# A two-block transformer step on one core: attention products turned round into two column groups, a reciprocal spread by a matmul, x read in four transfers, the constants waited for later

## The reference, cut to what matters

```
    def one_block(qblk):
        s = jnp.concatenate([jnp.einsum('bgrqd,bgkd->bgrqk', qblk, k),
                             jnp.einsum('bgrqd,bgcd->bgrqc', qblk, kc)], axis=-1)
        p = jax.nn.softmax(s.astype(jnp.float32) * scale, axis=-1).astype(v.dtype)
        return (jnp.einsum('bgrqk,bgkd->bgrqd', p[..., :length], v)
                + jnp.einsum('bgrqc,bgcd->bgrqd', p[..., length:], vc))
    ...
    y = _merge_heads(_dense_attention(q[:, :, None], k, v, kc, vc, MLA_SCALE)[:, :, 0]) @ w_out
```

## Time and profile before

| | us |
|---|---|
| median of 3 runs | 1869.68 (1869.36 to 1870.29) |
| the profiled execution | 1873.88 |
| its span between first and last instruction | 1872.0 |
| PE busy | 1694.2 (91%) |
| DVE busy | 951.4 (51%) |
| ACT busy | 743.0 (40%) |
| POOL busy | 101.9 (5%) |

### The profile page before, as it was taken

One profiled execution on the slowest core, in us unless ns is written; L12 is line 12 of the kernel. 1 busy time (PEld: TensorE's weight loads), 2 busy tenths in 40 slices (PEclk: granted clock), 3 DMA queues, 4 the chain that ended last, 5 costly groups with the idle time before them and its releaser, 6 DMA issues.

```text
span 1872.0 us, 36381 instructions
## 1 busy us (share of the span) xinstructions
PE 1694.2 (91%) x14713; PEld 1372.9 (73%) x14713; DVE 951.4 (51%) x1734; ACT 743.0 (40%) x1398; POOL 101.9 (5%) x158
## 2 busy tenths in 40 slices
PE   6888899897798887999998999999998799989997
PEld 6776578686566665877775887888786657779997
DVE  4743563476623224274555655245535555468584
ACT  5332434454111124224654433333326325565454
POOL 0020000004000001000002100000011000010000
PEclk9989899998899999999998999999998899989999
DMA  6597676668599997221002222323222310235552
GB/s 231 181 225 278 225 250 236 228 227 254 228 388 408 407 369 257 79 79 46 1 26 77 78 97 89 98 91 98 83 97 68 101 51 1 91 124 183 182 188 68
DMA packets 84799, 303.57 MB, mean 162 GB/s; under 512 B 10080, under 2 KB 12128, under 8 KB 84512
## 3 DMA queue, kind: packets, MB, share of 16 engines
q1 hardware_dynamic: 80576, 290.49, 44.3%
q0 software_dynamic: 2736, 7.35, 1.7%
q10 hardware_dynamic: 1328, 3.47, 0.5%
HBM read 347.14 MB, written 3.15 MB: 187 GB/s over the span
## 4 chain that ended last, share of the span: by engine, by line
PE 79%; DVE 9%; ACT 4%; DMA 4%; issue 4%; SPq 0%; ACTq 0%; DVEq 0%
PE bank L926 50%; PE bank L871 15%; PE bank L1403 4%; DMA ring<-wall 3%; PE bank L1438 3%; PE bank L1423 3%; PE bank L950 3%; DVE w_lo L2099 1%; ACT w_hi L1629 1%; DVE BIG L2722 1%; DMA con<-consts 1%; PE bank L1415 1%; PE bank L1459 1%; ACT BIG L1692 0%; DVE BIG L2395 0%
## 5 line engine op out<-in xcount | busy, mean ns | idle before, releaser
L926 PE MATMUL bank<-BIG_f32r,w_hi 128*128 128x256 f32 (+1 forms) x2208 | 550.7, 339 | 23.9 <-DVE BIG_f32r L2114 15.8
L2099 DVE TENSOR_TENSOR w_lo<-ring,w_hi 128x1024 fp32r<-128x1024 f32 x260 | 322.7, 1250 | 331.1 <-ACT w_hi L1629 329.7
L926 PEld LDWEIGHTS bank<-BIG_f32r,w_hi 128*128 128x128 f32 x2208 | 381.5, 192 | 73.6 <-issue 25.6
L926 PE MATMUL bank<-BIG_f32r,w_lo 128*128 128x256 f32 (+1 forms) x1136 | 385.9, 340 | 0.0
L1629 ACT ACTIVATE w_hi<-ring 128x1024 fp32r<-128x1024 f32 x260 | 271.3, 1053 | 223.2 <-PE bank L926 156.0
L926 PE MATMUL bank<-AR_f32r,w_hi 128*128 128x256 f32 (+1 forms) x1066 | 269.4, 331 | 16.8 <-issue 9.4
L926 PEld LDWEIGHTS bank<-BIG_f32r,w_lo 128*128 128x128 f32 x1136 | 217.8, 192 | 25.4 <-issue 0.2
L926 PEld LDWEIGHTS bank<-AR_f32r,w_hi 128*128 128x128 f32 x1066 | 185.7, 192 | 37.3 <-issue 9.8
L926 PE MATMUL bank<-AR_f32r,w_lo 128*128 128x256 f32 (+1 forms) x448 | 147.3, 329 | 0.0
L926 PE MATMUL bank<-lnst_f32r,w_hi 128*128 128x256 f32 x318 | 100.5, 316 | 31.0 <-DVE w_lo L2099 27.8
L926 PE MATMUL bank<-XC_f32r,w_lo 128*128 128x256 f32 x424 | 125.9, 297 | 0.0
(11 more groups left out here) (359 smaller groups left out, 2168.7 us busy)
## 6 DMA issues: line engine op xcount, KB each, us to landing
ring<-wall SPq DMA_DIRECT2D x454, 512.0 KB, 4.4
BIG<-wall SPq DMA_DIRECT2D x92, 512.0 KB, 10.2
w_extra<-wall ACTq DMA_DIRECT2D x15, 2048.0 KB
w_extra<-wall ACTq DMA_DIRECT2D x15, 1024.0 KB
BIG<-t_rows POOLq DMA_DIRECT2D x16, 128.0 KB, 12.7
AR<-na_rows POOLq DMA_DIRECT2D x32, 64.0 KB, 7.7
w_extra<-wall SPq DMA_DIRECT2D x1, 2048.0 KB
na_rows<-rpb_pad POOLq DMA_DIRECT2D x1, 1792.0 KB, 30.5
```

What stands on the lines that cost most here:

```text
L926: ins = nc.tensor.matmul(o, l, r, start=start and n == 0, stop=stop and n == 2, **kw)
L2099: V.tensor_tensor(w_lo[:, i % SPLIT_RING, :], ring[:, t % RING, :], w_hi[:, i % SPLIT_RING, :].bitcast(F32), ALU.subtract).then_inc(w_spli ...
```

## The change

Attention: for each pair PE now holds the values (128 keys by 64 columns) and moves the transposed probabilities (128 columns). Head 0 writes partitions 0 to 63 and head 1 partitions 64 to 127 of one bank, by `tile_position` (0, 0) and (0, 64), chunk by chunk in turn. The result has queries on the free axis, so Y, its banks and its transposes go. The reciprocal must then be spread over partitions: POOL multiplies the identity by each reciprocal (`diagonals`, two 128x128 instructions a pair), and PE multiplies ones by that diagonal into the second 128 columns of the same bank. DVE copies that half to SBUF, waits for its own copy, and multiplies O by it. In att1 this writes `ysT` directly; in att2 and att3 ACT makes the high part from SBUF, and DVE the low part one step later than before. The output projections wait for `y_low`.

Start: x comes in four transfers of 256 KB, each waited for on its own; SP starts tile 1 after the second. `consts_in` is waited for before `iwt` on PE and before the scan on DVE.

```diff
+            def diagonals(st):
+                diag = att1_diag if st == "att1" else att2_diag
+                for p in range(len(att_pairs[st])):
+                    gp_.wait_ge(sem("att_recip"), before_[st] // 2 + p + 1)
+                    if p >= 2:
+                        b, use = job[(st, "O", p - 2)]
+                        gp_.wait_ge(bank_ready[b], use)
+                    for q in range(2):
+                        nc.gpsimd.tensor_scalar(diag[:, (2 * p + q) % 4, :], c_("ident"),
+                                                SV[:, 80 + 2 * (p % 4) + q:81 + 2 * (p % 4) + q], None, ALU.mult)\
+                            .then_inc(sem("att_diag"), 1)
...
                     if 0 <= t - 2 < n:
                         b = open_((st, "O", t - 2))
-                        for q, s in enumerate(pairs[t - 2]):
+                        pe.wait_ge(sem("att_diag"), before_[st] + 2 * (t - 1))
+                        for q in range(2):
+                            mm(b[64 * q:64 * q + 64, P:2 * P], c_("ones")[:, 0:64], diag[:, (2 * t - 4 + q) % 4, :],
+                               tile_position=(0, 64 * q))
                             evacuated(pe, (st, "T", t - 2, q))
-                            for c in range(last + 1):
-                                mm(b[:, 64 * q:64 * q + 64], PT[:, (2 * t - 4 + q) % NP, c, :], s["v"][c], c == 0, c == last,
-                                   (st, "O", t - 2) if q and c == last else None)
-                    if t >= 3 and (t - 3) % per == per - 1:
-                        g = (t - 3) // per
-                        b = open_((st, "Y", g))
-                        evacuated(pe, (st, "O", t - 3))
-                        for c in range(per):
-                            transpose(b[:, c * P:(c + 1) * P], yt[:, g % 2, c, :], ident,
-                                      (st, "Y", g) if c == per - 1 else None)
+                        last = pairs[t - 2][0]["nk"] // P - 1
+                        for c in range(last + 1):
+                            for q, s in enumerate(pairs[t - 2]):
+                                mm(b[64 * q:64 * q + 64, 0:P], s["v"][c], PT[:, (2 * t - 4 + q) % NP, c, :], c == 0, c == last,
+                                   (st, "O", t - 2) if q and c == last else None, tile_position=(0, 64 * q))
...
-                        dve.wait_ge(sem("att_recip"), before_[st] // 2 + p + 1)
-                        for q in range(2):
-                            ins = V.tensor_scalar(yt[:, g % 2, p % per, qs], b[:, qs], rd, None, ALU.mult)
-                        frees(ins, (st, "O", p))
+                        R = (att1_R if st == "att1" else att2_R)[:, p % 2, :]
+                        step(V.tensor_copy(R, b[:, P:2 * P]))
+                        frees(V.tensor_tensor(o, b[:, 0:P], R, ALU.mult), (st, "O", p))
...
-            act.dma_start(X1, xin.rearrange("k p t -> p k t")).then_inc(sem("x_in"), 16)
+            for j in range(4):
+                act.dma_start(X1[:, 2 * j:2 * j + 2, :], xin[2 * j:2 * j + 2].rearrange("k p t -> p k t"))\
+                    .then_inc(x_landed[j], 16)
```

More of the change, by code:

```diff
@@ L377, in build @@
         att1_P = bA.take(NP, S)
-        att1_y = bA.take(2, 2, P)
-        c_at = bA.at
+        att1_diag = bA.take(4, P)
+        att1_R = bA.take(2, P)
+        c_at = bA.at - 2 * P
         bA.at = 8192
@@ L482, in build @@
         tq = aL.take(5, 512)
+        att2_R = tq[:, 0, 0:2 * P].rearrange("p (a b) -> p a b", a=2)
+        att2_diag = aL.take(4, P)
         tq2 = q0_sq[:, 0:5, :]
@@ L525, in build @@
         last_split_use = split_at[early["out", KC - 1]] + 1
+        x_landed = [sem(f"x_quarter_{j}_in") for j in range(4)]
         w_free = sem("ring_slots_freed")
@@ L801, in _ @@
             gp_.dma_start(scr_na, bass.AP(rpb_pad.tensor, 0, [[896, 8], [0, CH], [1, 896]])).then_inc(sem("na_rows"), 16)
+            diagonals("att1")
             gp_.wait_ge(sem("merged"), KC)
@@ L848, in _ @@
             new_x("b")
+            diagonals("att2")
             for which in "cde":
+                if which == "e":
+                    diagonals("att3")
                 z_total(which)
@@ L1663, in attention @@
                                   (st, "T", t - 1, q))
-                    if t >= 3 and (t - 3) % per == per - 1:
+                    if st != "att1" and t >= 3 and (t - 3) % per == per - 1:
                         g = (t - 3) // per
-                        b = bank(act, (st, "Y", g))[:, 0:per * P]
-                        if st == "att1":
-                            frees(f(ysT[:, g // 2, g % 2, :], b, ACT.Copy), (st, "Y", g))
-                        else:
-                            tell(f(y_hi[:, g, :], b, ACT.Copy), "y_high")
+                        evacuated(act, (st, "O", t - 3))
+                        tell(f(y_hi[:, g, :], att2_y[:, g % 2, 0:per, :].rearrange("p a b -> p (a b)"), ACT.Copy), "y_high")
                     if st == "att1" and t < NEAR:
@@ L1766, in beside @@
                         if m == 0:
-                            for g in range(4):
-                                evacuated(act, ("att1", "Y", g))
+                            for p in range(len(att1)):
+                                evacuated(act, ("att1", "O", p))
                         frees(f(gates[m][:, n, :], bank(act, ("gt", m, n))[:, 0:S], ACT.Copy), ("gt", m, n))
@@ L2140, in attention @@
                 n = len(pairs)
-                yt = att1_y if st == "att1" else att2_y
                 if st == "att3":
                     keys(0)
-                for t in range(n + 3):
+                for t in range(n + (3 if st == "att1" else 4)):
                     for q in range(2):
@@ L2160, in attention @@
                              "att_recip")
-                    if t >= 3:
+                    if st != "att1" and t >= 4 and (t - 4) % per == per - 1:
+                        g = (t - 4) // per
+                        evacuated(dve, (st, "O", t - 4))
+                        dve.wait_ge(sem("y_high"), (KC if st == "att3" else 0) + g + 1)
+                        tell(rest(lo[:, g, :], att2_y[:, g % 2, 0:per, :].rearrange("p a b -> p (a b)"), hi[:, g, :]), "y_low")
+                    if 3 <= t < n + 3:
                         p = t - 3
                         g = p // per
-                        if p % per == 0 and g >= 2:
-                            b, use = job[(st, "Y", g - 2)]
-                            dve.wait_ge(bank_ready[b], use)
                         b = bank(dve, (st, "O", p))
-                        dve.wait_ge(sem("att_recip"), before_[st] // 2 + p + 1)
-                        for q in range(2):
-                            qs = slice(64 * q, 64 * q + 64)
-                            rd = SV[:, 80 + 2 * (p % 4) + q:81 + 2 * (p % 4) + q]
-                            ins = V.tensor_scalar(yt[:, g % 2, p % per, qs], b[:, qs], rd, None, ALU.mult)
-                        frees(ins, (st, "O", p))
-                        if hi is not None and p % per == per - 1:
-                            b = bank(dve, (st, "Y", g))[:, 0:per * P]
-                            dve.wait_ge(sem("y_high"), (KC if st == "att3" else 0) + g + 1)
-                            frees(rest(lo[:, g, :], b, hi[:, g, :]), (st, "Y", g))
+                        if st == "att1":
+                            o = ysT[:, g // 2, g % 2, (p % per) * P:(p % per + 1) * P]
+                        else:
+                            o = att2_y[:, g % 2, p % per, :]
+                        R = (att1_R if st == "att1" else att2_R)[:, p % 2, :]
+                        step(V.tensor_copy(R, b[:, P:2 * P]))
+                        frees(V.tensor_tensor(o, b[:, 0:P], R, ALU.mult), (st, "O", p))
                     if st == "att1":
```

22 lines of the change are left out of this document (10 added, 12 removed).

## The result

The changed kernel takes 1847.41 us (median of 4 runs, 1846.55 to 1847.99) against 1869.99 (4 runs): a ratio of 0.988, 95% interval 0.986 to 0.990. It is faster by 22.6 us. The forecast was 37.1 us less, 1832.6; the time lies inside its range, but the terms of the sum have to be looked at one by one.

What follows compares the result with a forecast made beforehand. PE was taken to bound all three attentions. Att2 16.7, att3 12.6, ends 0.8, att1 2.0 and start 5.0 us sum to 37.1, taking 1869.7 to 1832.6 us; range 1824.6 to 1850.

Steps and rivals of the forecast that it cites:

- What bounds the kernel: All three attentions are bound by PE, 79% of the chain, with DVE nearest behind in the biased part of att2.
- Rival A: Column groups do not run side by side in the new O: slower, 1882 us; chance 5%.
- Rival B: DVE becomes the bound of att2, copy, handover and multiplication taking 1.3 us, not 0.65: time 1843.7 us; chance 12%.
- O in att2 and att3: New O on PE takes 0.87 us (512 keys) or 0.44 (256), diagonals 0.22: 2.37 us off four att2 pairs.
- What DVE does to att2: DVE gets 0.2 us more a pair; biased groups wait 1.1 us, taking 10.9, unbiased 9.8; att2 gives 16.7 us.
- Att3: PE stays far above the other engines; two pairs save 1.57 of 10.70 us, 12.6 us in all.
- ACT and POOL, ends: ACT stays under 9.8 us, POOL's diagonals (0.35 each) cost 0; ends of att2 and att3 give 0.6 and 0.2 us.
- Att1: Eight 256-key pairs save PE 3.2 us, partly lost to late weights: 2.0 us taken, bounds 0 and 3.5.
- The start: Before the attentions: x in pieces gives 2.0 us, constants' wait 1.7, clock staying up 1.3: 5.0, bounds 2 and 6.5.
- Rival C: The start gives little: x lands no sooner and PE's clock falls, 1.7 us instead of 5, time 1835.9; chance 30%.
- Sum: Whole kernel: 16.7 + 12.6 + 0.8 + 2.0 + 5.0 = 37.1 us less, a median of 1832.6.

Runs made afterwards that it cites:

- consts_only: Kernel before with the constants waited for where first read, x still in one transfer: 0.998 of the kernel before (0.996 to 0.999).
- batched3: Changed kernel with O of two pairs back to back in att3 alone, DVE's key copy behind reading O: 1842.76 us, 0.985 of before.
- split_d: Changed kernel with the diagonals' products moved ahead of the transposes in att2 and att3: att2 100.25 us (changed kernel 85.07), att3 80.82 (70.69).

## Why the prediction was right, and where its terms were not

- **What bounds the kernel.** Right: attention gained on PE, and the chain gives POOL 0%. Rival A was wrong: the records of the two heads start 6 to 7 ns apart, each with weights of its own. Rival B was wrong in its price, copy, handover and multiplication taking 0.60 us. The range, however, held in part by luck: its upper end of 1850 comes from rival B, and 1847.4 lies near it for another reason, the edges below.
- **O in att2 and att3, the mis-sized term.** The step that failed is the one from the layer norm to O: "15 steps take 0.82 us", and from this the new O at 0.87 and 0.44 and the diagonals at 0.22. The rate was right, but a group of records was priced by its inner distance, and its two edges were left out. PE's entry costs 0.093 us at the border and 0.05 at the next step, the exit 0.093 again, and 0.05 more for S in att3. In an unbiased group of att2 that is 0.236 x 4 = 0.94 us. Before had paid its own exits on the way to S (S there uses row groups, and followed O after 0.205 us before the change too). The forecast's 0.93 for O of a 256-key pair holds that exit; its 1.74 for 512 keys doesn't, where one such O took 1.83 up to the next S (897.27 to 899.10), so 0.09 comes off. That makes 0.85 of the 0.87 us by which the group, at 10.70, is above 9.83. In att3, where S is full-width too, it is 0.28 a pair, 0.57 in two, and the wait of 0.22 with it makes 0.8 of the 0.9 us that are missing. The rows that told it were in the trace of before: O to S in att2 stood 0.205 us apart, O to S in att3 0.112. The page "TensorEngine Tiling (Array Packing)" of the Trainium skill (Key Properties) says that changing the tiling mode drains the engine. The trace agrees in that the starts stand 0.202 us apart where the form changes and 0.109 where it doesn't. The page gives no price; the runs here show 0.2 to 0.4 us for one entry and one exit.
- **What DVE does to att2.** Right in kind. The extra of a biased group is 0.76 us (11.46 less 10.70), forecast 1.1. Together att2 gave 10.6 us, not 16.7.
- **Att3.** 4.5 us, not 12.6. Besides the edges, the forecast called DVE far from the bound because it was busy for about half the stage. Its order mattered: 1.39 us of copies ahead of the bank that PE wanted.
- **ACT and POOL, ends.** POOL's price was off by 0.28 us an instruction and cost nothing, 5.1 us of 10.7 being busy: a line through 512 and 256 columns doesn't reach down to 128, which take as long as 256. The two ends (0.6 and 0.2) can't be told apart: from the start of the last reduction of att3 to the end of the span there were 257.2 to 257.4 us in the four traces with the old attention and 255.2 to 258.0 in the nine with the new one, on average 0.9 less.
- **Att1.** Not settled. From its first to its last step it took 81.9 to 82.6 us in the four traces with the old attention and 79.1 to 82.9 in the nine with the new one, on average 1.2 us less; that fits the 2.0 forecast and fits half of it.
- **The start.** 5.4 us at 75 us against 5.0 (3.9 to 6.0 between other pairs of such traces at full clock), 3.9 by the whole time. The sum was right, partly by luck: x gave about 1.1 where it could be read and not 2.0 (tile 1 landed 1.1 us earlier, taking 3.98 us), and the constants with the clock 4.2 and not 3.0, the clock alone an estimated 2.7 by consts_only against batched3. Rival C was wrong here; batched3 shows that half of it, the falling clock, can happen.
- **Sum.** 10.6 + 4.5 + about 5 make 20.1, and with the averages of the ends and att1 (0.9 and 1.2) 22.2 of the 22.6 us. Of the shortfall of 14.5 us, 6.1 are att2 and 8.1 att3.

## What to carry to other kernels

Price a new group of matmuls with its edges: look in the trace for a place where the same kind of neighbours meet, and count the entries and exits a step, not only the records. Where column groups pay, gather their work behind one entry, as far as the engine that empties the banks can follow and the neighbours left behind need no change of their own: this gave 3.5 us in att3 (with DVE's order, 1.1 more) and lost 2.5 in att2, where DVE was near the bound and the step without O still went from full width to row groups. A busy share of one half doesn't say that an engine is out of the way; look at what it does ahead of the bank that is waited for.

## What the runs showed of the hardware that was not expected

- One change from full-width matmuls to column groups and back costs PE about 0.2 us beside row groups (0.24 by its edges, 0.21 by split_d) and 0.28 to 0.38 where all neighbours are full-width (edges, batched3, split_d), at a granted clock of 1.00. From full-width transposes to a matmul in row groups it is 0.203 us from start to start, as to column groups (0.202).
- Matmuls issued by head run partly side by side all the same: 1.46 us for 16 records, between 0.97 (taking turns) and 1.74 (O before the change, without column groups).
- POOL's multiplication by a scalar of each partition takes 0.59 to 0.61 us for 128 columns, where 256 take 0.600 and 512 take 1.096 in other stages. It takes 0.96 when it starts 0.17 us into a DVE instruction of 0.67 us with two inputs from SBUF, and 0.70 when it starts 0.18 us into one of 0.40.
- 1.00 us of idle time at the small products left the granted clock at 1.00 in nine runs and was followed by 0.55 in batched3; 2.58 us were followed by 0.59. By batched3 against consts_only the fall cost an estimated 2.7 us up to the chunk that is read near 70 us.
